# Decoder step: output weights of the mixer centred ahead of the second layer norm, and the third layer norm stored from inside the second dense half

## The reference, cut to what matters

```python
def layer_norm(x, g, b):
    mu = jnp.mean(xf, -1, keepdims=True)
    var = jnp.mean(jnp.square(xf - mu), -1, keepdims=True)
    return (xf - mu) * lax.rsqrt(var + LN_EPS) * g + b

x = layer_norm(ALPHA * x + 0.5 * swiglu_1(x), ln1_g, ln1_b)              # first dense half
x = layer_norm(ALPHA * x + concat(att, gdn) @ w_o, ln2_g, ln2_b)         # mixer: attention and delta rule
y = layer_norm(ALPHA * x + 0.5 * swiglu_2(x), ln3_g, ln3_b)              # second dense half, y is an output
```

## Time and profile before

| what | us |
|---|---|
| median of three runs (3086.74 to 3088.94) | 3087.49 |
| the profiled execution, whole | 3084.75 |
| its span, first to last instruction | 3083.1 |
| TensorE busy in it | 2798.6 (91%) |
| VectorE, ScalarE, GpSimd busy | 1523.5, 879.1, 227.1 |
| mean granted TensorE clock | 0.950 of full speed |

### The profile page before, as it was taken

The page is one execution under the profiler, slowest core; times in us unless marked ns, Lnnn a source line. Parts: engine busy times, 40 slices in busy tenths (PEclk is TensorE's granted clock), DMA queues, the critical chain, the costliest instruction groups (busy, mean ns, idle before and its releaser), DMA issues. The chain is left out here.

```text
span 3083.1 us, 44548 instructions
## 1 busy us (share of the span) xinstructions
PE 2798.6 (91%) x17330; PEld 2561.9 (83%) x17345; DVE 1523.5 (49%) x2400; ACT 879.1 (29%) x1450; POOL 227.1 (7%) x393
## 2 busy tenths in 40 slices
PE   7999999999949999968788788888879999999997
PEld 6999999999948799944688555468679999999997
DVE  5333333333454688837777588451453333333336
ACT  2111111111232567712355444441331111111111
POOL 0000000000000000005000000760000000000001
PEclk8999999999969999958899899999989999999998
DMA  3111111111031122234110101873011111111111
GB/s 108 55 42 42 42 47 43 47 50 35 8 111 35 43 71 78 85 85 111 42 52 11 54 15 32 233 209 113 14 48 49 54 42 41 48 41 48 41 41 58
DMA packets 264567, 186.69 MB, mean 61 GB/s; under 512 B 60303, under 2 KB 243807, under 8 KB 264390
## 3 DMA queue, kind: packets, MB, share of 16 engines
q1 hardware_dynamic: 212262, 112.33, 12.9%
q0 software_dynamic: 21440, 60.69, 6.0%
q10 hardware_dynamic: 30688, 11.27, 1.4%
HBM read 158.00 MB, written 26.22 MB: 60 GB/s over the span
## 5 line engine op out<-in xcount | busy, mean ns | idle before, releaser
L458 DVE TENSOR_TENSOR ffn_hidden<-ffn_hidden,ffn_ps_b 128x1092 f32<-128x1092 f32 x44 | 56.8, 1292 | 389.1 <-PE ffn_ps_b L85 389.1
L343 ACT ACTIVATE ffn_hi_d<-ffn_raw_d,ffn_row_mean 128x1024 fp32r<-128x1024 f32 x40 | 46.1, 1152 | 580.8 <-DVE ffn_row_mean L410 580.8
L359 ACT ACTIVATE ffn_h_hi<-ffn_hidden 128x1092 fp32r<-128x1092 f32 x44 | 49.2, 1119 | 485.5 <-DVE ffn_hidden L458 485.5
L205 POOL DMA_DIRECT2D ffn_raw_d<-in_ffn_w_down x40 | 21.2, 530 | 1590.4 <-DVE ffn_lo_d L419 1405.2
L85 PE MATMUL ffn_ps_a<-mixer_mix_hi,ffn_hi_g 128*128 128x364 f32 x528 | 117.8, 331 | 19.1 <-DVE ffn_lo_g L404 19.1
L85 PE MATMUL ffn_ps_a<-first_x_hi,ffn_hi_g 128*128 128x364 f32 x528 | 118.1, 332 | 10.2 <-DVE ffn_lo_g L404 5.9
L85 PE MATMUL proj_ps_a<-first_x_hi,proj_w_hi 128*128 128x364 f32 x336 | 78.9, 344 | 42.4 <-DVE proj_w_lo L1229 42.4
L85 PE MATMUL ffn_ps_a<-mixer_mix_lo,ffn_hi_g 128*128 128x364 f32 x528 | 117.2, 330 | 0.0
L85 PE MATMUL ffn_ps_a<-first_x_lo,ffn_hi_g 128*128 128x364 f32 x528 | 116.8, 330 | 0.0
L85 PE MATMUL ffn_ps_b<-first_x_lo,ffn_hi_u 128*128 128x364 f32 x528 | 116.6, 329 | 0.0
L85 PE MATMUL ffn_ps_b<-first_x_hi,ffn_hi_u 128*128 128x364 f32 x528 | 116.5, 328 | 0.0
(11 more groups left out here) (650 smaller groups left out, 6915.7 us busy)
## 6 DMA issues: line engine op xcount, KB each, us to landing
ffn_raw_d<-in_ffn_w_down POOLq DMA_DIRECT2D x40, 512.0 KB, 3.7
proj_raw<-in_w_in SPq DMA_DIRECT2D x22, 512.0 KB, 3.8
second_ffn_raw_g<-in_ffn_w_gate SPq DMA_DIRECT2D x22, 512.0 KB, 4.1
second_ffn_raw_u<-in_ffn_w_up SPq DMA_DIRECT2D x22, 512.0 KB, 5.0
first_ffn_raw_g<-in_ffn_w_gate SPq DMA_DIRECT2D x21, 512.0 KB, 3.8
first_ffn_raw_u<-in_ffn_w_up SPq DMA_DIRECT2D x21, 512.0 KB
scratch_qkv<-proj_stage POOLq DMA_DIRECT2D x12, 544.0 KB, 3.0
delta_cur<-scratch_qkv SPq DMA_DIRECT2D x8, 768.0 KB, 5.6
```

Source lines behind the costliest of these rows:

```text
L205: eng.dma_start(dst, src).then_inc(raw_in[kind], 16)
L343: act.activation(d_hi[:, k, :], raw["d"][:, :], ACT.Identity, bias=row_mean[:, k:k + 1]).then_inc(whi_done["d"], 1)
L359: act.activation(h_hi[:, par, fb, :], act_buf[:, fb, :], ACT.Copy).then_inc(hhi_done, 1)
L458: dve.tensor_tensor(hid, hid, ps_b[:, :, 0:SL], ALU.mult).then_inc(mul_done, 1)
```

## The change

In `ffn1`, GpSimd gets work behind its last down-weight load. It loads the 1024 rows of `w_o` in eight groups of 128, adds each row up by ten folding adds of halved width (512 down to 1), each waiting for the one before, divides by 1024, and leaves the means in `wo_means`. The next group is loaded when the one before is done.

`mixer_output` takes these means off each weight block before the split (`centre_rows`, VectorE), sums and centres the residual (seven adds, three means, three centrings), squares the finished blocks beside the product, does the last block slice by slice, and ends with the variances, the root and the spreading into `rstd`, as the first half does. `norm` is deleted; `ln2` becomes `apply_norm`, which now may leave out the store and do the early loads.

In `ffn`, both halves do their last block slice by slice, and `variances` takes the last block's squares ahead of the others. In `ffn2` the third norm moves inside: ScalarE multiplies the finished blocks by the gain column behind each square, TensorE turns three tiles at a time into the two free PSUM buffers, the first three tiles of the low half ahead of `variances`. VectorE does scale and bias in one instruction per half tile for seven of the nine tiles; for tiles 0 and 3 ScalarE scales and GpSimd adds the bias. Nine stores go out in the order 1, 2, 0, 4, 5, 3, 6, 7, 8. `store_norm` and its block are deleted.

```diff
 def ffn(...):
         @block.gpsimd
         def _(pool):
             load(pool, "d", 0, True)
             with pool.Fori(1, FB - 2) as n:
                 load(pool, "d", n, False)
+            if row_means is not None:
+                for k in range(KT):
+                    if k >= 1:
+                        pool.wait_ge(s["rows_meant"], k)
+                    parts = mixed_rows(k)
+                    for dst, src in parts:
+                        pool.dma_start(row_buf[dst, :], w_rows[0, src, :]).then_inc(s["rows_loaded"], 16)
+                    pool.wait_ge(s["rows_loaded"], 16 * sum(len(mixed_rows(j)) for j in range(k + 1)))
+                    width = D // 2
+                    while width >= 1:
+                        out = row_buf[:, 0:width] if width > 1 else w_means[:, k:k + 1]
+                        ins = pool.tensor_tensor(out, row_buf[:, 0:width], row_buf[:, width:2 * width], ALU.add)
+                        ins.then_inc(s["rows_folded"], 1)
+                        pool.wait_ge(s["rows_folded"], k * 10 + 11 - width.bit_length())
+                        width //= 2
+                    pool.tensor_scalar(w_means[:, k:k + 1], w_means[:, k:k + 1], 1.0 / D, None, ALU.mult
+                                       ).then_inc(s["rows_meant"], 1)
+            if store is not None:
+                pool.wait_ge(s["shift_in"], 32)
+                for n, t in enumerate(POOL_SHIFTS):
+                    pool.wait_ge(s["rows_act"], 2 * n + 2)
+                    pool.tensor_tensor(y_rows[t], y_rows[t], b_row[:, :], ALU.add).then_inc(s["shifted"], 1)
...
             def variances():
-                for part, squares in enumerate((total, act_buf[:, 1])):
+                for part, squares in ((1, act_buf[:, 1]), (0, total)):
...
             down(CHUNKS - 1, 0, last=True)
             pe.wait_ge(added_a, CHUNKS * 4)
+            if store is not None:
+                pe.wait_ge(s["weighted"], KT // 2)
+                turn(0, 0)
             variances()
+            if store is not None:
+                turn(0, 1)
+                for group in (1, 2):
+                    turn(group, 0)
+                    turn(group, 1)
...
+                    if last and m == KT - 1:
+                        for i in range(SLICES):
+                            dve.wait_ge(s["slice_filled"], i + 1)
+                            dve.scalar_tensor_tensor(r[:, i, :], ps_b[:, i, 0:SL], 0.5, r[:, i, :], ALU.mult, ALU.add
+                                                     ).then_inc(s["slice_added"], 1)
+                        sum_squares(m - 1)
+                        continue
...
-                    if last and 2 <= m < KT - 1:
+                    if last and m >= 2:
                         sum_squares(m - 1)
-                    if last and m == KT - 2:
-                        sum_squares(m)
...
+                    dve.wait_ge(s["inverted"], 1)
+                    for group in range(3):
+                        for half in range(2):
+                            part = slice(half * 512, half * 512 + 512)
+                            for t in range(3 * group, 3 * group + 3):
+                                if t in POOL_SHIFTS:
+                                    continue
+                                w = tile_width(t)
+                                if t == TILES - 1:
+                                    dve.wait_ge(s["first_out"], 16)
+                                dve.wait_ge(s["turned"], 6 * group + 3 * half + t % 3 + 1)
+                                dve.scalar_tensor_tensor(y_rows[t][0:w, part], (ps_b if half else ps_a)[0:w, t % 3, :],
+                                                         rstd_tok[0:w, t:t + 1], b_row[0:w, part], ALU.mult, ALU.add
+                                                         ).then_inc(s["rows_dve"], 1)
...
 def mixer_output(...):          # TensorE
+            for m in range(KT):
+                block_of(m)          # the last one slice by slice
+                if m == 1:
+                    residual_means((0, 1))
+                if m == 2:
+                    residual_means((2,))
+            variances()
...                              # VectorE
+            def centre_rows(m):
+                dve.wait_ge(s[f"raw_in{m % 2}"], 48 * (m // 2 + 1))
+                r = raw[:, m % 2, :].rearrange("p (k f) -> p k f", k=KT)
+                dve.tensor_tensor(r, r, w_means[:, :].unsqueeze(2).to_broadcast([P, KT, P]), ALU.subtract
+                                  ).then_inc(s["rows_centred"], 1)
...
+            centre_rows(0)
+            centre_rows(1)
             low(0)
             low(1)
-            dve.wait_ge(s["res_scaled"], KT)
+            for k in range(1, KT):
+                dve.wait_ge(s["res_scaled"], k + 1)
+                if k >= 2:
+                    dve.wait_ge(s["residual_summed"], k - 1)
+                dve.tensor_tensor(total[:, :], res[:, 0, :] if k == 1 else total[:, :], res[:, k, :], ALU.add
+                                  ).then_inc(s["residual_summed"], 1)
             for m in range(KT):
...
                 dve.wait_ge(s["filled"], m + 1)
+                if m == 2:
+                    dve.wait_ge(s["centred"], 2)
                 dve.tensor_tensor(r, r, ps[m % 2][:, :, 0:SL], ALU.add).then_inc(s["added"], 1)
                 if m + 2 < KT:
+                    centre_rows(m + 2)
                     low(m + 2)
+                if m == 1:
+                    dve.wait_ge(s["added"], 2)
+                    centre(0)
+                    centre(1)
...
 def decoder_step(...):
-                norm(nc, "ln2", a["ln2_g"], a["ln2_b"], ident, ones_mean, res, mix_hi, mix_lo,
-                     early=lambda eng, sem: load_first(eng, raws, a["ffn2_w_gate"], a["ffn2_w_up"], sem))
+                apply_norm(nc, "ln2", a["ln2_g"], a["ln2_b"], rstd, res, mix_hi, mix_lo,
+                           early=lambda eng, sem: load_first(eng, raws, a["ffn2_w_gate"], a["ffn2_w_up"], sem))
...
-            with nc.cleanup_on_exit():
-                store_norm(nc, "ln3", ident, g_row, b_row, rstd_tok, res, out["y_prompt"], out["y_sample"])
+                    store=(a["ln3_g"][0], a["ln3_b"], out["y_prompt"], out["y_sample"]))
```

More of the change, by code:

```diff
@@ L157, in load_first, with mixed_rows, rows_before, halves_before @@
     eng.wait_ge(sem, 32)
+def mixed_rows(k):
+    if k >= 4:
+        return [(slice(0, P), slice(k * P, (k + 1) * P))]
+    return [(slice(a * 64, a * 64 + 64), slice(a * 256 + k * 64, a * 256 + k * 64 + 64)) for a in range(2)]
+POOL_SHIFTS = (0, 3)
+STORE_ORDER = (1, 2, 0, 4, 5, 3, 6, 7, 8)
+def rows_before(t, own):
+    return sum((u in POOL_SHIFTS) == own for u in range(t))
+def halves_before(t, half, own):
+    g = t // 3 * 3
+    group = [u for u in range(g, g + 3) if (u in POOL_SHIFTS) == own]
+    return 2 * rows_before(g, own) + half * len(group) + group.index(t)
 def ffn(nc, name, w_gate, w_up, w_down, res, x_hi, x_lo, raws, ident, ones_mean, rstd_tok, rstd=None, weigh=False,
-        rows_in=()):
+        store=None, row_means=None):
     with ExitStack() as ctx:
@@ L711, in apply_norm @@
-def apply_norm(nc, name, g, b, rstd, res, x_hi, x_lo, resid_out):
+def apply_norm(nc, name, g, b, rstd, res, x_hi, x_lo, resid_out=None, early=None):
     with ExitStack() as ctx:
@@ L3189, in _, with block_of @@
         def _(pe):
+            def block_of(m):
+                pe.wait_ge(s["lo_made"], m + 1)
+                if m >= 2:
+                    pe.wait_ge(s["added"], m - 1)
+                hi = lambda k: w_hi[:, m % 2, k * P:(k + 1) * P]
+                lo = lambda k: w_lo[:, m % 2, k * P:(k + 1) * P]
+                if m < KT - 1:
+                    three_pass(pe, ps[m % 2], hi, lo, lambda k: mix_hi[:, k], lambda k: mix_lo[:, k], range(KT)
+                               ).then_inc(s["filled"], 1)
+                    return
+                for i in range(SLICES):
+                    c = slice(i * SL, i * SL + USED[i])
+                    for k in range(KT):
+                        for p, (w, x) in enumerate(((hi, mix_hi), (hi, mix_lo), (lo, mix_hi))):
+                            last = pe.matmul(ps[1][:, i, 0:USED[i]], w(k), x[:, k, c],
+                                             start=k == 0 and p == 0, stop=k == KT - 1 and p == 2)
+                    last.then_inc(s["slice_filled"], 1)
@@ new lines, in residual_means, with variances @@
+            def residual_means(parts):
+                for i in parts:
+                    if i == 0:
+                        pe.wait_ge(s["residual_summed"], KT - 1)
+                    if i == 2:
+                        pe.wait_ge(s["centred"], 1)
+                    pe.matmul(stat[:, i % 2, 0:SL], ones_mean[:, :], total[:, cols[i]], start=True, stop=True
+                              ).then_inc(s["mean_done"], 1)
+            def variances():
+                for part, squares in ((0, total), (1, sq[:, 1])):
+                    if part == 0:
```

(33 more changed lines are left out.)

426 lines of the change are left out of this document (160 added, 266 removed).

## The result

The changed kernel takes 3062.12 us (median of four runs, 3061.67 to 3064.63), the kernel before beside it 3087.11 us (3084.0 to 3088.94): a ratio of 0.9917 with a 95% interval of 0.9905 to 0.993, or 25.0 us less. The profiled execution took 3061.67 us with a span of 3060.0.

A forecast was written before the change was run, and what follows sets the result against it. TensorE, busy for 91% of the span, was taken as the bound. Terms -11.8 - 8.6 + 0.5 + 0.4 = -19.5 us took the profiled 3084.75 to 3065.3, and 2.7 for the median gave 3068.0; range 3063 to 3077.

The forecast's parts named there:

- Second norm: Stretch from the mixer's last product to the second half: 39.2 us in place of 58.0, so 18.8 less.
- down for both: Second norm: clock at 1.2 GHz for both variance groups, making product to scaling 17.4 us instead of 15.9.
- Mixer: Added sums and centring make TensorE start weight block 2 later: +7.0 us, bounds +6.1 and +8.5.
- Third norm: Kernel's end, last product to span's end: shorter norm, then stores decide; -8.6 us, bounds -10.5 and -6.
- First half and lock: Reordered variances at the first half's end, +0.5 us; GpSimd folds holding up VectorE through the shared port, +0.4.
- GpSimd's end: Eight groups of row means on GpSimd, 8.9 us each, end at 823, hidden behind the first half.
- The disputed price: Wait of each chained GpSimd fold: 0.25 us taken; rival 1, at 1.0 us, ends at 3103, chance 0.09.
- One sign that the prediction named: The prediction is wrong if the block after the first half starts later than 857.
- Second half, put at nothing: The second half's products: the forecast's sum has no term for them.
- the step from the terms to a time: Profiled 3084.75 less 19.5 gives 3065.3; the median lying 2.7 above that execution makes it 3068.0.

The follow-up runs named there:

- no_stop: The changed kernel with the mixer's steps reordered: weights of blocks 2 and 3 centred while VectorE waits for the residual; 3055.56 us, ratio 0.9895 to the kernel before.
- half_store: The changed kernel storing only the first 512 of the 1024 columns of y; the end takes 21.5 us.
- fold_twice: The changed kernel with GpSimd's loading and folding of the row means done twice over; 3132.15 us (one run).
- mixer_alone: The changed kernel with the last norm put back behind the second half as in the kernel before; 3075.96 us, ratio 0.9953 to the kernel before.
- no_stop_early: no_stop with the first group's pieces made row tile by row tile, so the first store is issued sooner; 3061.07 us, ratio 0.991 to the kernel before.

## Why the prediction was right in sign and outside its range

**Second norm, -18.8 forecast, -17.5 in the first pair of traces.** All steps came as written but one: the first variance group began 1.9 us behind the product (2.0 forecast), the scaling took 22.6, the change to the next half as before. The groups were forecast at 2.1 and 3.65 us and took 3.67 and 3.87, the clock granted there being 0.50, which is 1.2 GHz. That was the bound named for "down for both" (17.4 us to the scaling; 17.2 measured). Before its first group TensorE stood still for 1.92 us here and for 1.10 in the earlier trace rows.

**Mixer, +7.0 forecast, +6.2 and +5.9 by the means.** The mechanism is shown by no_stop. From the residual's landing to block 2's start 16.7 us pass, 16.9 by the forecast's steps. The size was less because the residual landed sooner, 24.7 us after the mixer's begin and not 26.2, which no term foresaw: 24.0 to 24.7 in the six traces with this order of steps, 25.4 to 26.3 in the four of before; no run tells why. The other way, the block after the stop took 14.6 us where 13.5 + 0.4 was forecast. Its size in one trace says little: it is 13.7 to 14.8 in those six traces and 12.2 to 14.9 in the four of before.

**Together** the two came to -11.3 in the first pair of traces, and to -12.6 by the means (-11.8 forecast): in the first pair a miss of +1.3 in the norm and one of -0.8 in the mixer nearly cancelled, which was luck. The kernel before has its second norm at 60.4 us in two of its four traces and at 62.2 in the two others; the prediction worked from one of the short ones.

**Third norm, -8.6 forecast, -9.5 in the pair, -9.1 by the means.** The reciprocal was ready after 7.7 us, not 9.3: squares and sums took 1.6 instead of 1.9, the variance groups 5.3 instead of 5.9, and nothing of the allowance above that was needed (the reciprocal came after 7.0 to 8.0 us in the other kernels with this end). The transfers took from 3046.8 to 3058.4, 11.6 us, inside the 10.9 to 12.8; the span's end followed 1.6 us behind them, not 0.9. half_store shows that the transfers were rightly put last, and by little.

**First half and lock, +0.9 forecast together, +1.1 by the means** (0.4 in the first pair). Half 1 lies anywhere from 851.7 to 856.0 us in the table, fold_twice aside, so the runs can't tell +0.9 from nothing. VectorE's two instructions shown above were stretched by 0.6 and 0.9 us where a fold ran, and TensorE's product was not later: 805.6 us in the first traces of both kernels. The Trainium skill (SBUF — State Buffer, Who interferes with whom) has VectorE instructions with two SBUF inputs and GpSimd's reads take turns at one port pair; the trace agrees, 1.92 against 1.28 us with and without the folds, and the other way too, 7.57 against 4.53 us for the folds. The store pieces, with an input in PSUM, take 0.73 to 0.75 us, the one at 3045.87 beside GpSimd's add too.

**GpSimd's end, 823 forecast, 839.6 measured.** The disputed price was right: nine folds without interference take 4.53 us, where 2.2 + 9 x 0.25 = 4.45 was put. What was missed: the first fold began 4.1 us later, at 760.07; three sets were held up by VectorE for 1.7, 1.8 and 3.0 us; and each group's multiply, waits and issues cost some 0.7 more than counted. It stayed hidden, so nothing hung on it. One sign that the prediction named did appear: the block after the first half issues its first transfer at 857.7, later than 857. It is at 855.1 in the kernel before, 2.1 us of the difference are the load's, and GpSimd had been done for 18 us.

**Second half, put at nothing, -1.0 measured.** All of it lies in the first hundred products, which take 18.3 us instead of 19.3; from there to the last product both kernels take 779.7. The granted clock rises sooner behind the new norm. The stretch from 4 to 6 us after the first product, before and after:

```profile
2254.73:2256.73 2.00, 2.00 (x8) 2.00 (x8) 1.79 (x3) 2.00 (x3) 0.00 (x0) 0.54 0.61 183
2242.14:2244.14 2.00, 2.00 (x14) 2.00 (x13) 1.78 (x3) 2.00 (x3) 0.00 (x0) 1.00 0.77 197
```

Ahead of that product TensorE had stood still for 19.1 us before and for 30.3 us after; what brings the clock up sooner stays open.

**The step that failed is the last one of the sum, the step from the terms to a time.** The time came out 5.9 us under the forecast. 2.3 us of it are the base: "the median of the runs lies 2.7 above that execution, so 3068.0" took a difference of the kernel before over to the new one, whose median lies 0.45 above its profiled execution in the first run and 0.9 below it in the second. 2.0 us are terms that the first pair of traces shows mis-sized: the third norm by 0.9, the second half, put at nothing, by 1.0, first half and lock by 0.5, less 0.5 in mixer and second norm. 1.6 us are load and middle, which the change doesn't touch and for which the sum had no scatter.

The difference in the base was not the chance of one execution. All four profiled executions of the kernel before lie below the median of the timed runs beside them, by 1.7 to 5.9 us; together they average 3085.1 us, its 37 timed runs 3089.0. The two profiled executions of the changed kernel average 3063.7 and its eight other runs 3064.1. Without that step the forecast was 3065.3, still 3.2 above the result but inside its range.

And the range held the bounds of the terms alone. They add up to -25.2 and -11.0, so by that base to 3062.2 and 3076.5, not 3063 and 3077. The untouched middle by itself moved between 1185.4 and 1194.8 us from one execution to the next, and the kernel before between 3082 and 3096 us; no end of the range had room for that. The middle of the first result's profiled execution was the shortest of all thirteen traces.

**What stays open.** About 3 us between the 25.0 and 23.8 of the timed runs and the traces' 21.4: the kernel before took some 4 us longer in its timed runs than in its profiled ones, the changed kernel hardly, and the executions that were only timed left no trace. The load of the tokens takes 38.3 to 39.8 us in all nine traces with any part of the change, and 36.6 to 37.7 in the four of before; the code is the same; no run here tells why.

## What to carry to other kernels

Work moved onto an idle engine is free as long as that engine ends before the block does, so price its end time and keep a margin: here 13 us, and past it each microsecond costs about one (65 us past it cost 67). When an added reduction makes TensorE wait, look first at the order of the steps in front of that wait: the mixer's 6 us came back by preparing the next weight block while the data for the reduction were still on their way. Add a term for the scatter of the stretches that the change doesn't touch, read from several executions, before a range is written down, and don't carry the difference between a profiled execution and the timed runs of one kernel over to another.

## What the runs showed of the hardware

TensorE's clock falls at another moment in each place and execution, and work put into the pause ahead of the variance groups did not visibly keep it up. At the end of the kernel twelve transposes follow the product at once, and the first group starts 0.27 us behind them; busy time and granted clock there, 1.00 being 2.4 GHz (stretches of the changed kernel):

```profile
3038.00:3040.00 2.00, 2.00 (x19) 1.97 (x19) 0.33 (x2) 1.69 (x2) 0.00 (x0) 1.00 0.00 0
3040.00:3042.00 2.00, 2.00 (x13) 2.00 (x13) 0.00 (x0) 0.00 (x0) 0.00 (x0) 0.61 0.00 0
```

The groups take 2.12 and 3.23 us. mixer_alone has no transposes there, and TensorE stands still for 1.58 us (its timeline and stretches):

```profile
3046.02 2.12 PE L360 MATMUL ffn_stat<-main_ones_mean,ffn_hidden 128*128 128x1 f32 x18 [1.58 <-ACT ffn_hidden L512]
3048.08 3.13 PE L360 MATMUL ffn_stat<-main_ones_mean,ffn_total 128*128 128x1 f32 x18
...
3046.00:3048.00 2.00, 1.98 (x18) 1.99 (x18) 0.54 (x1) 0.00 (x0) 0.00 (x0) 1.00 0.04 8
3048.00:3050.00 2.00, 2.00 (x15) 1.99 (x15) 0.17 (x1) 0.00 (x0) 0.00 (x0) 0.73 0.00 0
```

The groups are no slower, and the reciprocal is ready 7.7 us after the product in both. Behind the pause of 1.92 us in the mixer the groups took 3.67 and 3.87, the clock being at 0.50. But the length of the pause doesn't decide that alone: behind the same pause the first group took 3.3 to 3.8 us in the six traces with TensorE's stop behind block 1, and 2.22 and 2.83 in no_stop and no_stop_early; the second took 3.87 or 3.88 in all eight. No run isolates why.

The stores from SBUF run at 382 to 430 GB/s with nothing beside them, as long as SyncE has the next one to issue.
